# A two-block transformer kernel: the exponential-gate recurrence in one block, norm roots spread by a unit matrix

## The reference

```python
def rmsnorm_2(x, g, eps=1e-6):
    xf = x.astype(jnp.float32)
    y = xf * lax.rsqrt(jnp.mean(xf * xf, axis=-1, keepdims=True) + eps)
    return (y * g.astype(jnp.float32)).astype(x.dtype)
def modulate(x, g, shift, scale):
    return rmsnorm_2(x, g) * (1 + scale) + shift
```

```python
D = jnp.where(mask, bh[..., :, None] - bh[..., None, :] + igh[..., None, :], -jnp.inf)
m_t = jnp.maximum(D.max(-1), m_inter)
S = jnp.einsum('bthd,bshd->bhts', qc, kc) * jnp.exp(D - m_t[..., None])
...
h = num / jnp.swapaxes(jnp.maximum(jnp.abs(den), jnp.exp(-m_t)), 1, 2)[..., None]
```

## Time and profile before

| | us |
|---|---|
| median of 3 runs | 3631.76 (3628.35 to 3648.17) |
| profiled execution, its span | 3622.0 |
| PE busy | 3300.8 (91%) |
| PE weight load busy | 2830.7 (78%) |
| DVE busy | 2183.9 (60%) |
| ACT busy | 1453.4 (40%) |

### The profile page before, as it was taken

One profiled execution on the slowest core, in us unless ns is written; L12 is line 12 of the kernel. 1 busy time (PEld: TensorE's weight loads), 2 busy tenths in 40 slices (PEclk: granted clock), 3 DMA queues, 4 the chain that ended last, 5 costly groups with the idle time before them and its releaser, 6 DMA issues. The chain is left out here.

```text
span 3622.0 us, 54281 instructions
## 1 busy us (share of the span) xinstructions
PE 3300.8 (91%) x20534; PEld 2830.7 (78%) x20534; DVE 2183.9 (60%) x4214; ACT 1453.4 (40%) x2254; POOL 41.6 (1%) x66
## 2 busy tenths in 40 slices
PE   6987899999999798999999999699787999979897
PEld 4855799998888687999997888487555787857797
DVE  4523489875788635799767877424674433244553
ACT  3312444444554434444444454323233322233443
POOL 0000000000000000000000000000020000000000
PEclk7988999999999899999999999899997999979899
DMA  5465576556777635666567777322551233321353
GB/s 181 148 237 197 180 218 203 174 175 189 242 241 242 202 110 169 204 197 182 175 184 226 242 243 227 114 91 71 209 191 47 80 95 92 93 60 51 118 167 122
DMA packets 225065, 596.60 MB, mean 165 GB/s; under 512 B 27424, under 2 KB 97440, under 8 KB 224576
## 3 DMA queue, kind: packets, MB, share of 16 engines
q1 hardware_dynamic: 220656, 588.17, 52.1%
q10 hardware_dynamic: 4176, 5.29, 0.5%
HBM read 558.16 MB, written 35.19 MB: 164 GB/s over the span
## 5 line engine op out<-in xcount | busy, mean ns | idle before, releaser
L2489 PE MATMUL ps<-h_split,split_layer 128*128 128x256 f32 x6144 | 775.9, 286 | 9.4 <-DVE split_layer L2278 9.4
L2489 PEld LDWEIGHTS ps<-h_split,split_layer 128*128 128x128 f32 x6144 | 750.1, 193 | 11.9 <-DVE split_layer L2278 11.9
L2635 PE MATMUL ps<-split_layer,h_split 128*128 128x512 f32 x3072 | 701.1, 391 | 13.9 <-DVE h_split L2619 13.9
L2635 PEld LDWEIGHTS ps<-split_layer,h_split 128*128 128x128 f32 x3072 | 579.6, 189 | 134.9 <-DVE split_layer L2602 14.2
L779 PE MATMUL ps<-h_parts_ffn,split_ffn 128*128 128x512 f32 (+1 forms) x2112 | 383.1, 342 | 14.6 <-DVE split_ffn L731 8.1
L779 PEld LDWEIGHTS ps<-h_parts_ffn,split_ffn 128*128 128x128 f32 x2112 | 331.7, 193 | 67.4 <-issue 17.4
L2278 DVE TENSOR_TENSOR split_layer<-ring,split_layer 128x1024 fp32r<-128x1024 f32 x256 | 312.4, 1222 | 80.6 <-ACT split_layer L2417 79.1
L731 DVE TENSOR_TENSOR split_ffn<-ring,split_ffn 128x1024 fp32r<-128x1024 f32 x132 | 161.1, 1225 | 255.2 <-ACT split_ffn L706 246.8
L2602 DVE TENSOR_TENSOR split_layer<-ring,split_layer 128x1024 fp32r<-128x1024 f32 x256 | 313.7, 1225 | 0.0
L2425 ACT ACTIVATE kept_layer<-ps 128x256 f32<-128x256 f32 x256 | 98.4, 385 | 460.3 <-PE ps L2489 460.2
L2584 ACT ACTIVATE split_layer<-ring 128x1024 fp32r<-128x1024 f32 x256 | 267.5, 1045 | 4.5 <-PEq L467 4.5
(11 more groups left out here) (619 smaller groups left out, 3815.5 us busy)
## 6 DMA issues: line engine op xcount, KB each, us to landing
ring<-in_experts SPq DMA_DIRECT2D x512, 512.0 KB, 3.8
ring<-in_mod SPq DMA_DIRECT2D x96, 512.0 KB, 4.6
ring<-in_ada SPq DMA_DIRECT2D x96, 512.0 KB, 4.4
ring<-in_ffn_in SPq DMA_DIRECT2D x88, 512.0 KB, 3.6
hidden_layer<-kept_layer SPq DMA_DIRECT2D x256, 128.0 KB, 2.0
x_sb<-hidden_layer SPq DMA_DIRECT2D x256, 128.0 KB, 3.8
ring<-in_ffn_out SPq DMA_DIRECT2D x44, 512.0 KB, 3.7
ring<-in_peer_q SPq DMA_DIRECT2D x32, 512.0 KB, 3.6
```

The lines of the kernel that those rows point to most:

```text
L2489: ins = nc.tensor.matmul(ps[:, 4 + j % 2, 0:T], w[:, part, c], self.hsplit[:, moving, k, :], start=(k == 0 and n == 0), stop=(k == KT - 1 ...
L2635: ins = nc.tensor.matmul(ps[:, 2 * t + h, :], wsplit(j, a)[:, t * P:(t + 1) * P], w[:, b, h * 512:(h + 1) * 512], start=(j == 0 and n == 0 ...
```

## The change

- `mlstm` becomes one block, ordered by semaphores. Scores are made once per head. The row term is split in two F32R halves and spread by one product. Only diagonal tiles go through DVE (`cap`, with an additive mask); the rest goes from PSUM through ACT's exponential with the key term as bias. Forward and backward sums are normalised each and added on PE (`turn`). There are three buffers of weights, and 4 groups are hosted instead of 8.
- The gates are one chain of 8 products with 128 columns.
- Of the four groups that `mlstm` gives up, one is hosted by `GatedExit`, two by `add_streamed` behind it, one by the entry of ffn_0; `ORDER` follows.
- Norm roots: ACT's square root reads the counts in PSUM with eps as bias (`mean_root`), DVE inverts, and PE spreads the root as broadcast weights times the unit matrix (`widen_root`). The diagonals and the unused products go.
- `add_streamed` has no folds: PE counts all 8 tiles of squares as they come. The root for a counted entry is made at its end, and such an entry begins with scaling; the low half of its first unit comes behind the first scaled part.
- `linear_normed` squares before it copies, with a semaphore of its own.

```diff
     def scalar_root(self, act):
...
-        act.wait_ge(c.inverted.sem, self.at[c.inverted] + 1)
-        s.activation(self.root, self.root, ACT.Sqrt).then_inc(c.rooted.sem, 1)
+        c = self.core
+        act.wait_ge(c.entry_counted.sem, self.at[c.entry_counted] + 1)
+        c.mean_root(self.root, c.ps[:, 5, 0:self.nt], D).then_inc(c.rooted.sem, 1)
...
     def vector_root(self, dve):
...
-        dve.wait_ge(c.entry_counted.sem, at[c.entry_counted] + 1)
-        at0 = 16 if self.counted else 0
-        v.tensor_scalar(self.root, ps[:, 5, at0:at0 + self.nt], 1.0 / D, EPS, ALU.mult, ALU.add).then_inc(done.sem, 1)
...
-        v.reciprocal(self.root, self.root).then_inc(c.inverted.sem, 1)
+        c, at = self.core, self.at
         dve.wait_ge(c.rooted.sem, at[c.rooted] + 1)
-        for t in range(self.nt):
-            ins = v.tensor_scalar(self.spare[:, t * P:(t + 1) * P], c.ident, self.root[:, t:t + 1], None, ALU.mult)
-        ins.then_inc(c.diagonals.sem, 1)
+        c.nc.vector.reciprocal(self.root, self.root).then_inc(c.inverted.sem, 1)
...
-        elif self.warm and not self.counted:
-            turn(7)
...
+        if self.counted:
...
-        elif self.warm and not self.hosted:
-            turn(4)
-        pe.wait_ge(c.diagonals.sem, at[c.diagonals] + 1)
-        mm(ps[:, 6, 0:self.n], c.ones, self.spare, start=True, stop=True).then_inc(c.widened.sem, 1)
+        pe.wait_ge(c.inverted.sem, at[c.inverted] + 1)
+        c.widen_root(ps[:, 6, :], self.root, self.nt).then_inc(c.widened.sem, 1)
...
+            if k == 0 and between is not None:
+                between()
...
+    def host(self, jobs):
+        c = self.core
...
+        self.banks, self.hosted = (4, 5, 6, 1, 2), 1
...
         c.rows_turn(pe, n_c, m0, m1, bank)
+        if self.hosted:
+            c.aside_products(pe, 0, 8)
...
+            if m >= 2:
+                nc.scalar.wait_ge(added.sem, added0 + m - 1)
+            nc.scalar.activation(squares[:, m % 2, :], x[:, 0:n], ACT.Square).then_inc(self.result_squared.sem, 1)
             for j, (cols, g) in enumerate(parts):
                 at = slice(cols.start - c0, cols.stop - c0)
-                nc.scalar.activation(y[:, m, at], x[:, at], ACT.Copy, scale=col[:, j, m:m + 1])
-            if m >= 2:
-                nc.scalar.wait_ge(added.sem, added0 + m - 1)
-            return nc.scalar.activation(squares[:, m % 2, :], x[:, 0:n], ACT.Square)
+                ins = nc.scalar.activation(y[:, m, at], x[:, at], ACT.Copy, scale=col[:, j, m:m + 1])
+            return ins
...
-                mm(ps[:, 7, 0:T], self.ones, total[:, 0:T], start=True, stop=True)
-                pe.wait_ge(diagonals.sem, at[diagonals] + 1)
-                mm(ps[:, 6, 0:n], self.ones, diagonal, start=True, stop=True).then_inc(widened.sem, 1)
+                pe.wait_ge(inverted.sem, at[inverted] + 1)
+                self.widen_root(ps[:, 6, :], root[:, 0, :], nt).then_inc(widened.sem, 1)
+                if jobs:
+                    self.aside_products(pe, 0, 8)
                 if counted:
-                    pe.wait_ge(self.squared.sem, at[self.squared] + QUARTERS)
-                    for i in range(3):
-                        mm(ps[:, 7, 0:T], self.ones, total[:, 0:T], start=True, stop=True)
-                    pe.wait_ge(folded.sem, at[folded] + QUARTERS)
-                    for t in range(nt):
-                        ins = mm(ps[:, 5, 16 + t:17 + t], squares[:, 0, t * P:(t + 1) * P], self.ones[:, 0:1],
-                                 start=True, stop=True)
+                    for k in range(KT):
+                        if k % per == 0:
+                            pe.wait_ge(self.squared.sem, at[self.squared] + k // per + 1)
+                        for t in range(nt):
+                            ins = mm(ps[:, 4, t:t + 1], squares[:, k, t * P:(t + 1) * P], self.ones[:, 0:1],
+                                     start=(k == 0 and t == 0), stop=(k == KT - 1), skip_group_check=True)
+                        if jobs and k == KT // 2 - 1:
+                            self.aside_products(pe, 8, 8 * len(jobs))
                     ins.then_inc(counts.sem, 1)
+                    pe.wait_ge(inverted.sem, at[inverted] + 2)
+                    self.widen_root(ps[:, 6, :], root[:, 1, :], nt).then_inc(widened.sem, 1)
...
-                    if counted and i >= 3:
...
-                        a, b = fold(i - 2)
-                        v.tensor_tensor(a, a, b, ALU.add).then_inc(folded.sem, 1)
                 if counted:
...
-                    a, b = fold(QUARTERS - 1)
-                    v.tensor_tensor(a, a, b, ALU.add).then_inc(folded.sem, 1)
...
-                    v.tensor_tensor(squares[:, 0, :], squares[:, 0, :], squares[:, 1, :], ALU.add).then_inc(folded.sem, 1)
+                    dve.wait_ge(rooted.sem, at[rooted] + 2)
+                    v.reciprocal(root[:, 1, :], root[:, 1, :]).then_inc(inverted.sem, 1)
...
+                self.mean_root(root[:, 0, :], ps[:, 5, 0:nt], D).then_inc(rooted.sem, 1)
+                if jobs:
+                    self.keep_row(act, 0)
                 if counted:
                     for i in range(QUARTERS):
                         act.wait_ge(summed.sem, at[summed] + i + 1)
                         part = slice(i * per, (i + 1) * per)
                         nc.scalar.activation(squares[:, part, :], x[:, part, :], ACT.Square).then_inc(self.squared.sem, 1)
...
+                        if i == 2:
+                            for j in range(1, len(jobs)):
+                                self.keep_row(act, j)
+                    act.wait_ge(counts.sem, at[counts] + 2)
+                    self.mean_root(root[:, 1, :], ps[:, 4, 0:nt], D).then_inc(rooted.sem, 1)
...
+                    for j in range(len(jobs)):
+                        self.fetch_group(sp, j)
+                        self.store_row(sp, j)
+                    sp.wait_ge(self.row_stored.sem, stored0 + sum(16 * job[3] for job in jobs))
...
+    def mean_root(self, out, sums, n):
+        return self.nc.scalar.activation(out, sums, ACT.Sqrt, bias=self.eps, scale=1.0 / n)
+    def widen_root(self, out, root, nt):
+        for t in range(nt):
+            ins = self.nc.tensor.matmul(out[:, t * P:(t + 1) * P], root[:, t:t + 1].broadcast_to([P, P]), self.ident,
+                                        start=True, stop=True)
+        return ins
...
-                for g in range(2):
-                    for k in range(KT):
-                        ins = nc.tensor.matmul(ps[0:W, 4 + g, :], c["gates"][:, k, g * W:(g + 1) * W], self.hT[:, k, :],
-                                               start=(k == 0), stop=(k == KT - 1))
+                for k in range(KT):
+                    ins = nc.tensor.matmul(ps[:, 4, :], c["gates"][:, k, :], self.hT[:, k, :],
+                                           start=(k == 0), stop=(k == KT - 1))
...
+                for d in range(2):
+                    v.tensor_scalar(c["tri"][d], c["tri"][d], -1.0, -NEG, ALU.add, ALU.mult)
...
+                v.tensor_copy(halves[0:W, :], tmp).then_inc(done.sem, 1)
+                after()
+                v.tensor_tensor(halves[W:P, :], tmp, halves[0:W, :].bitcast(F32), ALU.subtract)
...
+        first = [0, 0, TC, TC]
+        seen = [[[(j * P, TA)] for j in range(NT)],
+                [[(0, P), (TC, TA)], [(0, TA)], [(TC, TC + P)], [(TC, TA)]]]
+        beside = [[(0, P, TA), (1, 2 * P, TA), (2, 3 * P, TA)], [(1, 0, P), (0, TC, TA), (1, TC, TA), (3, TC, TC + P)]]
...
+                def rows(n):
+                    if n:
+                        pe.wait_ge(weighed.sem, at[weighed] + n)
+                    if n >= 4 and n % 2 == 0:
+                        pe.wait_ge(moved.sem, at[moved] + n // 2 - 1)
+                    nc.tensor.matmul(ps[:, 6, :], pick[:, n % 2 * HEADS + n // 2, :], halves, start=True, stop=True
+                                     ).then_inc(rows_made.sem, 1)
+                def scores(h):
+                    half = slice(h % 2 * 64, h % 2 * 64 + 64)
+                    for j in range(NT):
+                        if h:
+                            pe.wait_ge(multiplied.sem, at[multiplied] + NT * (2 * h - 1) + j + 1)
+                        nc.tensor.matmul(ps[:, 2 + j, first[j]:TA], qk[half, 2 + h // 2, j * P:(j + 1) * P],
+                                         qk[half, h // 2, first[j]:TA], start=True, stop=True).then_inc(scored.sem, 1)
+                def totals(n, ts):
...
+                    if ts[0] == 0:
+                        pe.wait_ge(multiplied.sem, at[multiplied] + NT * (n + 1))
+                        if n:
+                            pe.wait_ge(normed.sem, at[normed] + n)
+                    for t in ts:
+                        keys = keys_of(d, t)
+                        for j in keys:
+                            ins = nc.tensor.matmul(both[:, t // 2, t % 2, :], weight(n)[:, j, t * P:(t + 1) * P],
```

(68 more changed lines are left out.)

## The result

The changed kernel takes 3589.05 us (median of four runs, 3584.26 to 3596.0); the kernel before, run beside it, 3631.35 (median of four). The ratio is 0.9891 with an interval of 0.9869 to 0.9914, that is 42 us less. The profiled execution of the changed kernel took 3587.6 us and its span is 3585.9, so what lies around the span is 1.7 us. Against the 3622.0 of the trace of before, the spans differ by 36.1 us; the prediction's sum for the same difference was 35.0.

The account below looks back on a forecast made before the run. The prediction took PE as the bound, with a barrier paid on top of each `mlstm` item. Its terms summed to -35.0 us against the 3622.0 span; with 9.8 carried for the median, 3597, range 3583 to 3617.

Parts of the forecast that it names:

- A: `mlstm` stage: PE's work is the bound, 58.6 us instead of 87.1, so -28.5 us (ends -32 and -20).
- B: Gates: 16 records of 128 weight columns take half the time of 32 with 64, -6.9 us.
- C: `GatedExit` with a hosted group: hosted products may raise the clock for the products behind, -1.5 us (-3.3 to +1.5).
- D: `add_streamed` behind the recurrent stage and ffn_0's entry: slow counting and hosted groups delay the first product, +5 us (+1.9 to +10).
- E: Addition behind ffn_0, without hosted groups: counts end 4.6 us later, the entry gives back 3.1, +1.5 us (-1.5 to +2).
- F: Addition with 256 columns behind the grouped attention: half the records and DVE steps, -1.3 us (-2.5 to 0).
- H: `linear_normed`: squaring ahead of the gated copies ends DVE's sum earlier at four places, -1.8 us (-2.5 to 0).
- I: Other norms (start, block two, latent): lose a DVE step and the diagonals on a bare chain, -1.2 us (-2 to 0).
- The first: Rival: PE keeps the low clock through `mlstm`, stage about 100 us, whole 3638, slower than before; chance 0.05.
- The second: Rival: moved groups wait full 4.4 us landings at group 10, group 11 and ffn_in's unit 0, whole 3615; chance 0.12.
- The third: Rival: hand-overs between engines, not PE, bound `mlstm`; stage 65 to 76 us, total 3604 to 3615; chance 0.15.
- The fourth: Rival: counting products run at the fast clock, 0.11 us a record instead of 0.215, whole 3591; chance 0.10.

Follow-up runs that it names:

- the larger comparison: The changed kernel timed again with no edit: 3585.88 us (median of six) against 3626.64 for the kernel before (median of eleven), ratio 0.9889.
- half groups: Changed kernel with F32R counting and three hosted groups moved to the values stage, two units ahead of each of six value tiles: 3571.84 us, ratio 0.9845.
- whole ones: Changed kernel with three whole hosted groups moved to the values stage, each ahead of a value tile: span 3612.8 us.

## Why the prediction was right, and where it was off

The forecast was 3597 with a range of 3583 to 3617, and the time is 3589.05.

- **A** (forecast -28.5, measured -30.0): the stage takes 57.2 us where 58.6 was forecast, a head 12.1 where PE's sum was 12.3, PE busy 53.1 where 49.2 and the cold start's 2.8 make 52.0; the eight executions with this `mlstm` take 55.5 to 57.2. The terms that had no row were near: 0.47 to 0.51 for a row (which overlaps its successor by 0.16) instead of 0.22, 2.05 for the turn instead of 2.0, 2.84 for the scores instead of 2.93. Of the 3.5 for waits at hand-overs little is seen. The four prices that erred went both ways.
- **B** was exact; the old form, put back, costs 5.3 of the 6.9, the rest being the four pairs that overlap there.
- **C** (-1.5, measured 0.0) assumed that hosted products raise the clock for L394's successor. They ran at 1.00 themselves, but the narrow products behind them fell to 0.50 while PE was busy. Its 16 records took 12.65 instead of 13.44, and the sum of squares ahead lost as much (9.97 where 9.19 was measured before).
- **D** (+5, measured +8.1, and +5.8 to +8.7 over the five traces with this code) is the term that was mis-sized, within its ends. In this trace the counting was priced right (0.215 a record at a clock of 0.50; in three of the five half of the records had 0.12), and the block began 6.4 us later where 9.7 was forecast, since squares and counts of the first parts lay beside each other and beside group 10. The failing step is "its scaling then starts at once". The condition's columns that group 11 multiplies lie in the tile of the first scaled part (`pad = work[:, 0, :]`), so DVE waits 3.76 until PE has read them, and then ACT waits 1.30 more for unit 0 of ffn_in, which was asked for only when group 11's first pair was used. The landing ends last, as L742 shows: DVE was done with the first part at 2779.04 and waits 2.03 for ACT. Then my second correction, that finished parts let PE run without the pace of before, can't be judged: ffn_0 takes 379.3 us before, 378.8 in this trace and 376.5 to 377.3 in the ten others, with and without the hosted groups, and between the two traces of the changed kernel it is the clock that differs.
- **E** (+1.5, measured -0.1): the shorter entry gave back all that the counts cost, where I had taken half. **F** and **G** came out as forecast, **H** as -2.0 instead of -1.8, though its part at ffn_1 is larger and at the out product nothing; the out product's stretch scatters from 46.9 to 48.3 and ffn_0's as said, so that the sum is no confirmation. What **I** gives can't be told from the scatter of the first 2440 us; at the norm 18 us into the kernel it is 0.65 (3.48 us from the counts to what DVE does with the root before, 2.83 after), at that of the latent layer 0.25.
- **The sum** of the parts, -35.0, met the -36.1 of the traces. The forecast is 8 us too high by the step behind it: "the median stands 9.8 above that span, and I carry the same 9.8". What lies around a span is 1.7 us here. The profiled execution of before, about 3623.7 by that, was one of the faster ones: other runs of that kernel gave 3618.13 to 3648.17. The 9.8 was scatter, read as something constant outside the span; 3622.0 - 35.0 + 1.7 would have been 3588.7. That this meets the median within 0.4 is partly chance, since the traces of the changed kernel scatter as well. Carrying the 9.8 comes to taking 35.0 off the median of before, and from median to median the gain was 42.3 and 40.8. So the sum may also be some 6 us short; the intervals (33 to 47 us in the larger comparison) leave both open.

The rivals. The first (low clock through `mlstm`) fell with the 1.00 of the windows from 2520 on. The second (bare landings) came true in one of its three places: unit 0 of ffn_in; group 10's units were there. The third (hand-overs bound the stage) did not come, but with the cap twice its chain showed only 0.6 us of slack a head. The fourth (counting at the fast clock) fell in the result's trace, and behind ffn_0 in all seven traces that have these 64 records: PE is busy all of 13.8 us at a granted clock of 0.50. But behind group 10 it came half true in three of five traces, with 0.12 a record at 1.00, so that "narrow products don't get the fast clock here" was too strong. The sentence of the Trainium skill that the prediction weighed, in its page "TensorE: Matmul & The Clock Gate", section "Part 1: The HAM clock gate", that activity releases the throttle, is borne out by the dense products of `mlstm` and not by the 64 behind ffn_0.

What stays open: why the counts behind group 10 run at the fast clock in three executions and not in two, what ends the addition where they do, and how much of the 42 us between the medians is more than the 36 between the traces.

## What to carry to other kernels

When a stage becomes shorter, the work that it hosts for others has to move with its transfers: count the ring's slots that the host leaves free, and cut the guest to that size (half groups cost 7.1 us where whole ones cost 28.7). Price narrow fp32 products by records, not by columns, and at both levels of the clock, since records of one form were seen at either. Before a stretch is read to a microsecond or two, look at it in a second trace of the same code: ffn_0 moved by 2.2 us with nothing changed in it. Compare span with span when a sum is made from a trace, and look where a hosted step's scratch lies before letting the stage behind it begin at once.

## What the runs showed of the hardware

- Products can keep PE busy without a gap and still be granted 0.50: 64 records of one moving column (13.81 us), and 16 records that are 8 rows deep (12.65 us), though the hosted group ahead of these ran at 1.00. Records of the first kind also ran at 1.00: 32 of them behind a hosted group took 3.9 to 4.0 us in three of five executions of the same code, 6.99 in the other two.
- A weight load of 128 x 128 takes 333 ns at a granted clock of 0.50 for fp32 and for F32R; an fp32 product with one moving column is two records of 0.215 us there, an F32R product with two is one of 0.22 to 0.23.
- Records of 512 moving columns start 0.43 us apart with 64 weight columns and with 128. Two chains of the former that write different halves of the partitions overlapped by four records where one ended and the other began.
- The same 2440 us of code end up to 14 us apart in eleven profiled executions, at mean granted clocks of 0.940 to 0.947 over the span. A gain under that is read from stretches of the trace, not from the end.
